# A two-layer encoder trunk on TensorE: first norm's sums, constants, weight roundings and an opening run of matmuls moved

## What is computed

```python
def _layer(x, ...):
    h = _rms(x, attn_norm[l])
    z = h @ w_in[l]                       # q, k, v of the differential heads, c_q, c_kv, k_pe
    ...
    y_diff = _diff_attention(dq, dk, dv, lam, diff_subln[l], lam_init)
    qh = _rms(c_q, q_a_norm[l]) @ w_q_b[l]
    kvh = _rms(c_kv, kv_a_norm[l]) @ w_kv_b[l]
    ...
    y_mla = _mla_attention(q_nope, q_pe, k_nope, k_pe, v)
    x = x + jnp.concatenate([y_diff, y_mla], axis=-1) @ w_o[l]
    h = _rms(x, ffn_norm[l])
    return x + (jax.nn.silu(h @ w_gate[l]) * (h @ w_up[l])) @ w_down[l]

def _trunk(x, ...):
    for l in range(2):
        x = _layer(x, pos, l, ...)
    return _rms(x, final_norm)
```

## Time and profile before

| | |
|---|---|
| median of 3 runs | 2431.84 us (2429.0 to 2432.96) |
| the profiled execution | 2434.94 us, its span 2432.9 us |
| granted TensorE clock, mean | 0.989 |
| busy: TensorE, VectorE, GpSimd, ScalarE | 97%, 72%, 35%, 32% of the span |
| TensorE busy, 0 to 65 us | 47.15 us |
| TensorE busy, 65 to 162 us | 93.53 us |
| TensorE busy, 162 to 200 us | 33.47 us |
| DMA | 266.91 MB, mean 110 GB/s |

### The profile page before, as it was taken

The page is one execution under the profiler, slowest core; times in us unless marked ns, Lnnn a source line. Parts: engine busy times, 40 slices in busy tenths (PEclk is TensorE's granted clock), DMA queues, the critical chain, the costliest instruction groups (busy, mean ns, idle before and its releaser), DMA issues.

```text
span 2432.9 us, 32372 instructions
## 1 busy us (share of the span) xinstructions
PE 2359.5 (97%) x11064; PEld 1954.2 (80%) x11064; DVE 1749.1 (72%) x3037; ACT 768.4 (32%) x1491; POOL 841.1 (35%) x636
## 2 busy tenths in 40 slices
PE   7989999999999999999999999999999999999996
PEld 5877888878888888888788888878788888888875
DVE  5888388867777666676758874897666666666677
ACT  4456134522222222222224532454222222222212
POOL 4213100157666666663300010003544444444421
PEclk9999999999999999999999999999999999999998
DMA  8533442253333333331332135223211111111112
GB/s 286 204 104 130 173 172 81 88 190 130 130 128 119 117 127 122 125 115 44 138 139 104 59 133 208 104 87 130 87 53 52 52 52 52 52 52 52 52 52 95
DMA packets 55680, 266.91 MB, mean 110 GB/s; under 512 B 6560, under 2 KB 6688, under 8 KB 37536
## 3 DMA queue, kind: packets, MB, share of 16 engines
q1 hardware_dynamic: 54864, 264.83, 31.1%
q10 hardware_dynamic: 720, 0.86, 0.1%
HBM read 196.45 MB, written 69.21 MB: 109 GB/s over the span
## 4 chain that ended last, share of the span: by engine, by line
PE 78%; DVE 9%; issue 4%; ACT 2%; POOL 1%; DMA 0%; DVEq 0%; ACTq 0%; SPq 0%; POOLq 0%
PE bank L478 25%; PE bank L479 24%; PE bank L480 24%; DVE x L1771 3%; PE bank L976 2%; DVE u_lo L1757 1%; PE bank L817 1%; DVE silu L1747 1%; POOL w L686 1%; ACT w L1395 1%; PE bank L825 1%; DVE qpe L1594 0%; DMA raw<-in_wffn 0%; POOL w L681 0%; PE bank L485 0%
## 5 line engine op out<-in xcount | busy, mean ns | idle before, releaser
L478 PE MATMUL bank<-h_hi,w 128*128 128x512 f32 x1792 | 703.9, 393 | 6.9 <-issue 6.3
L480 PE MATMUL bank<-h_hi,w 128*128 128x512 f32 x1792 | 699.4, 390 | 0.0
L479 PE MATMUL bank<-h_lo,w 128*128 128x512 f32 x1792 | 699.2, 390 | 0.0
L1771 DVE TENSOR_TENSOR x<-x,bank 128x512 f32<-128x512 f32 x768 | 471.0, 679 | 5.1 <-PE bank L480 3.4
L686 POOL TENSOR_TENSOR w<-raw,w 128x512 fp32r<-128x512 f32 x230 | 331.6, 1465 | 285.0 <-ACT w L1315 123.2
L478 PEld LDWEIGHTS bank<-h_hi,w 128*128 128x128 f32 x1792 | 337.6, 188 | 77.0 <-issue 7.1
L480 PEld LDWEIGHTS bank<-h_hi,w 128*128 128x128 f32 x1792 | 337.6, 188 | 71.0
L479 PEld LDWEIGHTS bank<-h_lo,w 128*128 128x128 f32 x1792 | 337.9, 189 | 69.1
L738 POOL TENSOR_TENSOR wd<-down_raw,wd 128x512 fp32r<-128x512 f32 x120 | 163.0, 1367 | 487.1 <-ACT wd L1388 487.1
L478 PE MATMUL bank<-u_hi,wd 128*128 128x512 f32 x560 | 221.8, 396 | 9.8 <-DVE x L1771 4.4
L479 PE MATMUL bank<-u_lo,wd 128*128 128x512 f32 x560 | 219.6, 392 | 0.0
(11 more groups left out here) (206 smaller groups left out, 3962.8 us busy)
## 6 DMA issues: line engine op xcount, KB each, us to landing
w<-parked SPq DMA_DIRECT2D x81, 1024.0 KB, 4.8
raw<-in_wffn SPq DMA_DIRECT2D x88, 512.0 KB, 3.5
parked<-w SPq DMA_DIRECT2D x27, 1024.0 KB, 6.6
parked<-p SPq DMA_DIRECT2D x27, 1024.0 KB, 4.8
down_raw<-in_wffn SPq DMA_DIRECT2D x44, 512.0 KB, 3.6
raw<-in_watt SPq DMA_DIRECT2D x27, 512.0 KB, 4.7
praw<-in_watt SPq DMA_DIRECT2D x27, 512.0 KB, 5.7
x_kept<-x SPq DMA_DIRECT2D x4, 2048.0 KB, 9.1
```

The costliest lines, as they stand in the source:

```text
L478: nc.tensor.matmul(out_ap, lhs[0], rhs[0], start=first, stop=False)
L479: nc.tensor.matmul(out_ap, lhs[0], rhs[1], start=False, stop=False)
L480: return nc.tensor.matmul(out_ap, lhs[1], rhs[0], start=False, stop=last)
L1771: nc.vector.tensor_tensor(xn, xn, bank[banks + m][:], op).then_inc(s_acc.sem, 1)
```

## The change

Four things are done; the second batch and layer 1 keep their order.

1. TensorE waits for the tile of ones and multiplies it 14 times by itself into bank 6, which nothing reads, before it waits for chunk 0.
2. ScalarE copies one column of ones first, with its table load ahead of that copy; its DMAs of `lam` and `cs` are issued behind the rounding of chunk 2.
3. In layer 0 the sums of the first norm stand between chunks 2 and 3 of the values, and no longer behind chunk 3.
4. ScalarE's roundings move: chunk 3 to a place between squares 5 and 6; chunks 4 and 5 stay ahead of the values; 6 goes ahead of `RH q0`, 7 and 8 ahead of `RH k0`, 9 ahead of `RH q1`, 17 ahead of `LC cq1`, 18 ahead of `TH 12`.

```diff
-FIRST_ROUNDS = {"V": [3, 4, 5, 6], "RH q0": [7, 8], "RH k0": [9], "TH 0": [10], "EX 3": [11], "TH 3": [12], "RH q3":
-    [13], "TH 6": [14], "TH 7": [15], "TH 10": [16], "TH 12": [17], "PH kn0": [18], "TH 17": [19], ...
+FIRST_ROUNDS = {"V": [4, 5], "RH q0": [6], "RH k0": [7, 8], "TH 0": [10], "EX 3": [11], "TH 3": [12], "RH q3": [13],
+    ... "TH 31": [24], "SN 6": [25], "SN 7": [26], "LC cq1": [17], "TH 12": [18], "RH q1": [9]}
...
             def first_values():
+                pe.wait_ge(s_pre, 1)
+                for _ in range(14):
+                    nc.tensor.matmul(bank[6][:, 0:P], ones[:], ones[:], start=True, stop=True)
                 pe.wait_ge(s_hi.sem, s_hi.half_at(0, 0, 0))
...
+                    if l == 0 and b == 0 and j == 3:
+                        pe.wait_ge(s_pre, 2)
+                        norm_sums("first", 0)
                     wc = chunk(l, b, j)
...
                             if l == 0 and b == 0:
                                 pe.wait_ge(s_load, 4 * 16)
-                                pe.wait_ge(s_pre, 2)
-                            if b == 0:
+                            if b == 0 and l:
                                 norm_sums("first", l)
...
+            act.wait_ge(s_pre, 1)
+            nc.scalar.activation(rc[:, 0:1], ones[:, 0:1], ACT.Copy)
             act.dma_start(ident[:], tables[:, 2 * T:2 * T + P]).then_inc(s_load, 16)
             act.dma_start(masks[:], tables[:, 2 * T + P:2 * T + P + 4]).then_inc(s_load, 16)
             act.dma_start(gsmall[:], gains[:, g.shape[1]:]).then_inc(s_load, 16)
-            act.dma_start(lamt[:], lam).then_inc(s_load, 16)
-            act.dma_start(cs[:], tables[:, 0:2 * T].rearrange("p (a t) -> p a t", a=2)).then_inc(s_cs, 16)
...
             first_hi(2)
+            act.dma_start(lamt[:], lam).then_inc(s_load, 16)
+            act.dma_start(cs[:], tables[:, 0:2 * T].rearrange("p (a t) -> p a t", a=2)).then_inc(s_cs, 16)
             for k in range(KT):
                 norm_square("first", 0, 0, k)
+                if k == 5:
+                    slot_hi(WS_ATT)
```

More of the change, by code:

```diff
@@ L114 @@
 """)
-FIRST_ROUNDS = {"V": [3, 4, 5, 6], "RH q0": [7, 8], "RH k0": [9], "TH 0": [10], "EX 3": [11], "TH 3": [12], "RH q3":
-    [13], "TH 6": [14], "TH 7": [15], "TH 10": [16], "TH 12": [17], "PH kn0": [18], "TH 17": [19], "EX 23": [20], "EX 25":
-    [21], "TH 22": [22], "EX 30": [23], "TH 31": [24], "SN 6": [25], "SN 7": [26]}
+FIRST_ROUNDS = {"V": [4, 5], "RH q0": [6], "RH k0": [7, 8], "TH 0": [10], "EX 3": [11], "TH 3": [12], "RH q3": [13],
+    "TH 6": [14], "TH 7": [15], "TH 10": [16], "TH 17": [19], "EX 23": [20], "EX 25": [21], "TH 22": [22], "EX 30": [23],
+    "TH 31": [24], "SN 6": [25], "SN 7": [26], "LC cq1": [17], "TH 12": [18], "RH q1": [9]}
 STATS = [s[1] for s in TENSOR_ORDER if s[0] == "RB"]
```

## The result

The changed kernel takes 2417.77 us (median of 4 executions, 2413.72 to 2418.64); the kernel before, beside it, took 2430.42 (4 executions, 2428.52 to 2432.96). The ratio is 0.9937, 95% interval 0.9925 to 0.995: **faster by 12 to 18 us**. A later batch timed both again: 2418.29 (5 executions) against 2432.78 (10), ratio 0.9942, interval 0.9928 to 0.9956. The forecast was 16.9 us less, 2415 for the median. By the medians the gain is 12.7 us in the first batch and 14.5 in the later one, so the forecast was some 2 to 4 us too high; the 16.4 us between two single executions flatter it, since that of the kernel before lay 3.1 us above its median of three.

A forecast was written before the change was run, and what follows sets the result against it. TensorE, busy 97% of the span, was taken as the bound. Gains 9.2 + 2.5 - 0.7 + 5.9 = 16.9 us gave 2418.0 us for an execution like the profiled one and 2415 for the median, range 2409 to 2424.

The forecast's parts named there:

- 0.79 MB / 329 GB/s = 2.4: Start: constants taken out ahead of raw chunk 1 make its rounding 2.4 us earlier, bounds nothing and 3.3.
- The zero: Start: matmuls on ones gain nothing, covered by chunk 1's arrival; without that cover 1.8 us.
- Sums and chunk 3: First norm: spread of rstd 6.8 us earlier, scaled tables 2.4 more, so first scores 9.2 us earlier.
- The contention: Last additions of squares: VectorE slowed beside GpSimd's low part of chunk 3, 1.2 us taken, bounds 0 and 1.3.
- Clock at the scores: Behind the first scores: a shorter wait lets the clock stay high, 2.5 us gained.
- Rival A: Low clock returns after shorter waits: 2.1 to 2.5 us a stretch; one at the scores 2417.5, two 2420; chance 0.14.
- Rival B: Chunk supply becomes the wait: raw chunk 8 holds `kd_hi`, first scores 3.7 us later and slow; 2421 us; chance 0.14.
- a loss of 0.7: Before `qd_hi` of q1: chunk 9's rounding, moved ahead, delays it by 1.15 us, partly absorbed; 0.7 us lost.
- Chunks 17 and 18: Ahead of `kn0`: 4.33 us wait and 2.1 us slow stretch go, 0.5 lost; 5.9 us gained, bounds 3.4 and 6.4.
- C: After 65 us: VectorE is the bound, 12 or more of 16.9 us given back; 2427 to 2433 us; chance 0.07.
- D: Loops: instruction supply makes each of 18 passes begin with a 3.2 us wait; 54 us more, 2469; chance 0.05.

The follow-up runs named there:

- b: The change with the `lam` and `cs` DMAs issued at the head of ScalarE's queue again; 2418.12 us, ratio to the kernel before 0.9934.
- g: The kernel before with only `lam` and `cs` issued behind the rounding of chunk 2; 2431.03 us, ratio 1.0004.
- e: The kernel before with only the 14 products of ones added; 2432.22 us, ratio 1.0003.
- f: The kernel before with only the roundings of chunks 17 and 18 moved to their new places; 2428.55 us, ratio 0.999.
- h: The kernel before with only chunk 3's rounding moved between squares 5 and 6; 2429.54 us, ratio 0.9993.
- c: The change with the first norm's sums behind chunk 3 again; 2418.97 us, ratio to the kernel before 0.9943.
- i: The change with the roundings of chunks 6 to 9 at their old places; 2423.48 us, ratio to the kernel before 0.9965.
- d: The change with chunks 17 and 18 rounded at their old places; 2420.99 us, ratio to the kernel before 0.9943.
- j: The change with chunk 17 rounded behind the latent copies again, ahead of chunk 18 and `TH 12`; 2417.60 us, ratio to the kernel before 0.9941.
- a: The change without the 14 products of ones; 2416.94 us, ratio to the kernel before 0.993.
- l: The change itself, run and profiled once more; 2418.29 us, ratio to the kernel before 0.9942.

## Why the prediction was right

**Start.** Raw 1's rounding at 10.93 and chunk 1 at 15.25 stand 0.3 and 0.15 us from the forecast, but the term "0.79 MB / 329 GB/s = 2.4" was too large. At the rounding of chunk 1 kernel b prices it at 0.7 us, and g against e, f and h at 1.8 to 1.9; at chunk 1 on TensorE it is 0.7 and 0.8 to 1.0, all within the bounds given. That the forecast times came out is in part luck: the 13.61 from which it counts was itself 0.9 to 1.0 us later than in e, f and h. The three small transfers did not queue behind the table load: they were issued from 1.75 on, as before. The Trainium skill, DMA: Bandwidth & Descriptors, "Issuing engines are not separate DMA queues", says that DMAs started by ScalarE and SP run on the same 16 engines and interleave. That raw chunk 1 comes later in b than in the change fits it; how much of the delay falls on which transfer it does not say.

**Ones.** The zero held, with its cover: they ran from 2.03 to 7.4 (forecast 1 to 7), and chunk 1 came at the same time with and without them. Their price, at a place where TensorE would only wait, was zero too; in kernel e a half-clock stretch came behind them, which no timing shows.

**Sums and chunk 3.** Sums at 27.32 (27.5), chunk 3 at 28.21 (28.5), `q0` at 33.78 (33.9), spread at 39.22 (39.4), tables taken up at 39.92 (40.0). The contention was there, but its term was too small: two additions beside GpSimd took 3.16 us, 1.6 more than the 1.56 of two alone, against 1.2 taken and a bound of 1.3. The sums came on time all the same because the four `x_lo` took 4.33 us in place of the 5.38 counted.

Two readings in between were off. `rstd` was to finish by 34, and came at 36.2: the 128x4 steps of the rsqrt chain stalled four times for about a microsecond beside GpSimd's 5.18 us. ScalarE therefore still waited for it, 3.96 us. It cost nothing at the spread, which had to stand behind `q0` anyway. In the other direction, S0 came at 51.68 and not 52.7, because `qd_lo` took 1.42 us in place of 2.98. Before, chunk 8 was rounded just ahead of `qd_hi`, and GpSimd's low part of it (53.63, 3.00 us) lay over `qd_lo`; now 7 and 8 are both rounded behind `qd_hi`, and GpSimd begins at 46.75, when `qd_lo` is over. The prediction looked at what the roundings hold up on ScalarE, not at what their low parts hold up on VectorE.

**Clock at the scores.** 2.5 us were expected behind S0 and came: the earlier trace rows had 14 matmuls in 5.70 us at 0.50, and after has 1.00 there. Kernel c shows that it was near: 2.08 us of wait brought the slow stretch back. Rival A's mechanism is real: it came in c at the scores, and in the change itself, at 142.7, for 0.78 us.

**Chunk supply.** Rival B did not happen, since raw chunk 8 came 0.33 us late and with 1.80 us to spare. Kernel i shows what it would have been. The prediction had no term for the moves of 6 to 9 but a loss of 0.7. They are worth 5.4 us, hidden in the step from the spread to S0. So the sum was right there because it was taken from milestones of the trace, while its split over the edits was not. The loss at chunk 9 can't be seen: from S0 (10.2 us earlier) to the sums of cq at 139.55 (12.4 earlier) the change gains 2.1, against 2.5 - 0.7 = 1.8.

**Chunks 17 and 18.** The wait went as forecast, but the term is 4.0 us instead of 5.9, within its bounds of 3.4 to 6.4. The stretch from the start of cq's sums to S16 takes 23.46 us before (from 151.91) and 19.44 after (from 139.55), in three pieces:

| piece | before | after | gain | forecast |
|---|---|---|---|---|
| sums of cq to their spreading | 5.72 | 6.70 | -0.98 | -0.5 |
| spreading to `kn0` | 7.79 | 4.24 | 3.55 | 4.33 |
| `kn0` to S16 | 9.95 | 8.50 | 1.45 | 2.1 |

The first piece is not so much the square held up by chunk 17 as the contention again. VectorE's 128x4 steps of cq's rsqrt chain, kernel d (17 and 18 as before):

```profile
142.65 1.21 DVE L1542 TENSOR_SCALAR yy<-yi 128x4 int32<-128x4 int32 x1
143.89 0.16 DVE L1545 TENSOR_TENSOR ms<-yy 128x4 f32<-128x4 f32 x1
```

the changed kernel:

```profile
142.20 1.21 DVE L1542 TENSOR_SCALAR yy<-yi 128x4 int32<-128x4 int32 x1
143.45 1.18 DVE L1545 TENSOR_TENSOR ms<-yy 128x4 f32<-128x4 f32 x1
```

and kernel j:

```profile
142.07 1.21 DVE L1542 TENSOR_SCALAR yy<-yi 128x4 int32<-128x4 int32 x1
143.32 1.18 DVE L1545 TENSOR_TENSOR ms<-yy 128x4 f32<-128x4 f32 x1
144.53 1.19 DVE L1546 SCALAR_TENSOR_TENSOR ms<-ms,ms 128x4 f32<-128x4 f32 x1
```

One long step, two and three; the piece takes 5.73, 6.70 and 7.78 us. GpSimd makes the low parts of 17 and 18 in that time, 4.60 of the 5 us from 140 on. In d only chunk 17's low part lies over the chain (141.09 to 143.83), in the change both do until 144.60, in j both until 145.70, and each stretch takes in one step more.

The second piece lost 0.78 us to the clock: the forecast took all of it at full clock. TensorE of the changed kernel, where it fell:

```profile
142.52 0.28 PE L478 MATMUL bank<-aT_hi,v_hi 128*128 128x256 f32 x1
...
142.76 0.42 PE L480 MATMUL bank<-aT_hi,v_lo 128*128 128x256 f32 x1
```

In the change, b, f and i the clock is low before the wait, in a, c and l (the same order here) only behind it, where it is 2.8 us long; `kn0` comes within 0.1 us at the same time in the change and in l. With 17 and 18 in their old places (d and before) the wait is 1.90 us, and the clock stays. The third piece was over-counted: the 11 instructions of the earlier trace rows were priced as if all ran 0.227 us apart at full clock, 2.1 us of gain. The twelfth came 4.81 us behind `kn0` before and 2.99 now, a gain of 1.8, and short pauses further on (0.3 us at 152.6, 0.2 at 157.2) leave 1.45.

**From 200 us on.** TensorE carried the gain to the end, 16.4 us, so rivals C and D did not happen: no pass begins with a wait that adds up, and S16 to the end is the same 2257.5 us as before. In between it looked smaller, 14.8 us at 410, because a half-clock stretch near 230 was longer than its like before (granted clock 0.83 over 220 to 240 us, against 0.91 over 240 to 260). A later one of the kernel before, with 0.91 over 1700 to 1720, is missing here (1.00), and the distance between the two executions grows there from 14.6 to 16.4 us.

**The sum.** Undone one by one, the parts are worth at S16: ones nothing, constants 2.9 (about half of it a half-clock stretch in b), sums 2.6, 6 to 9 5.4, 17 and 18 4.0, together 14.9 of the 16.4 us. By medians, each against the change or its stand-in a in the same batch, they are worth 1.2, 2.0, 5.2 and 4.0, together 12.4 of 12.7 to 14.5; only the last two stand out of the scatter, and barely. So the forecast of 16.9 was high, and the two terms that carried it were the constants (2.4) and chunks 17 and 18 (5.9). Done one by one on the kernel before, ones, constants, chunk 3, and 17 and 18 shift the median of 2430.39 by +1.8, +0.6, -0.9 and -1.8 us, together next to nothing. The rival "one edit alone" falls: none of these four gives it, and i, which lacks only the largest part, is still 9.3 us faster than the kernel before. What 6 to 9, or the sums, give alone on the kernel before, and what chunk 3's place is worth inside the change, was not tried.

## What to carry to other kernels

When several hand-ordered queues feed one bound engine, read the next two waits behind the one that you remove: here four edits that alone moved the median by less than 2 us each were parts of a change worth 13 to 15. Place a rounding (or any load-bound step) behind the work that is already ready, and check which engine its follow-up will contend with. Warming matmuls buy nothing if what they speed up then waits for the next input (and the clock may fall in that wait, as in e), and single profiled executions should be compared from milestone to milestone, since starts differ by a microsecond.

## What the runs showed of the hardware

- **Tiny VectorE instructions stall as long as one of GpSimd's.** The 128x4 steps took 0.16 or 0.17 us alone and 1.2 beside GpSimd's subtractions of 1.3 us each (5.18 us for four). The chain for the first norm had four such stalls in the change, and ScalarE waited for its end; that for cq had one, two or three (d, the change, j), and TensorE waited for it. The Trainium skill, SBUF — State Buffer, "Who interferes with whom", says that the engine that issues second blocks until the other's instruction is over; the rows of 1.2 us fit that, also for steps with one input.
- **The clock can fall without a wait before it.** In the change it fell at 142.7, with TensorE at work since the 16 products of 128x1 began at 139.55 and no wait in between; in l, the same program, those matmuls stayed at 0.28 us and the clock was low only behind a wait of 2.78 us.
- **Wait lengths do not sort cleanly by the clock.** Behind 2.13 us ahead of chunk 1 (b) it stayed at 1.00, behind 2.19 at the same place (e) it fell, behind 2.08 (c) too, and in b the first matmuls of chunk 3 were slow behind a wait of 1.56 us and the small products of the sums (granted clock 0.79 over 28.7 to 36.7 us).
- **Half-clock stretches differ between executions of one program.** The change ran from 140 to 145 us at a granted clock of 0.77 in one execution and 1.00 in the other. The span from S16 to the end is 2254 to 2258 us for fourteen profiled executions, with 2257.5 for the first of the change (mean clock 0.990) and 2258.0 for the second (0.992), so the mean clock alone does not tell it; that and the start are of the size of the 3 to 8 us by which the runs of one kernel scatter.
- **Transfers on ScalarE's queue delay those of SP, by less than their bytes over the bandwidth**: with 0.79 MB issued ahead on it, SP's next chunk came 0.7 us later (b against the change) or 1.8 to 1.9 (e, f and h against g), where 329 GB/s gives 2.4. These are single executions, whose starts differ by up to a microsecond.
